# A Mixture-of-Experts Kernel: the First Pair of Expert Blocks Picked on TensorE Instead of Gathered from Memory

## The reference

```python
h = layer_norm(ALPHA * h + mixed, ln_g[i, 0], ln_b[i, 0])
ffn = hierarchical_moe(h, ...)              # 32 experts, top 2 of the chosen group of 8
h = layer_norm(ALPHA * h + ffn, ln_g[i, 1], ln_b[i, 1])
# inside hierarchical_moe, for the rows xb that chose expert e:
hb = silu(xb @ w_gate[e]) * (xb @ w_up[e])  # 1024 -> 512
y  = hb @ w_down[e]                         # 512 -> 1024
# y times its gate is added to the token's row
```

## Time and profile before

| what | value |
|---|---|
| median of 3 runs | 2321.19 us (2316.19 to 2324.91) |
| span of the profiled execution | 2316.0 us |
| mean granted TensorE clock | 0.955 of full speed |
| instructions | 28602 |
| TensorE matmul busy | 2117.5 us (91%) |
| DMA | 545.97 MB, mean 236 GB/s |
| expert blocks of layer 0 begin at | 1029.46 us of the span |
| expert blocks of layer 1 begin at | 1797.52 us of the span |

### The profile page before, as it was taken

How to read it: one execution, slowest core, us unless ns; L and a number is a source line. 1 busy time by engine, 2 the same in 40 slices (tenths; PEclk the granted TensorE clock), 3 DMA queues, 4 the chain that set the end, 5 groups by cost and what they waited for, 6 DMA issues and landing times. The chain is left out here.

```text
span 2316.0 us, 28602 instructions
## 1 busy us (share of the span) xinstructions
PE 2117.5 (91%) x11642; PEld 1217.9 (53%) x11642; DVE 693.5 (30%) x1536; ACT 539.4 (23%) x1241; POOL 253.4 (11%) x270
## 2 busy tenths in 40 slices
PE   7999999999999999969999899869996999989991
PEld 3446743434445687445555454457754555545550
DVE  1054325343555455542111010151125211101104
ACT  2123221033663145112221121130001212121111
POOL 0000000210101210101111111130000111111101
PEclk9999998999999999969999999979997999999996
DMA  9315242222011222169999999962034999999993
GB/s 348 125 59 186 85 181 94 78 105 73 1 56 58 91 77 76 35 241 406 423 424 423 423 423 417 389 244 98 30 125 177 373 422 425 423 423 423 423 407 141
DMA packets 100665, 545.97 MB, mean 236 GB/s; under 512 B 13377, under 2 KB 27498, under 8 KB 66587
## 3 DMA queue, kind: packets, MB, share of 16 engines
q1 hardware_dynamic: 80950, 504.17, 54.0%
q0 software_dynamic: 19232, 39.56, 4.8%
q10 hardware_dynamic: 340, 0.28, 0.0%
HBM read 538.86 MB, written 28.94 MB: 245 GB/s over the span
## 5 line engine op out<-in xcount | busy, mean ns | idle before, releaser
L759 PE MATMUL ps<-arena,ring 128*128 128x512 f32 (+8 forms) x1888 | 555.6, 456 | 11.1 <-DVE arena L2254 2.2
L759 PEld LDWEIGHTS ps<-arena,ring 128*128 128x128 f32 x1888 | 344.6, 193 | 212.8 <-issue 173.2
L1262 PE MATMUL ps<-ring,arena 128*64 128x256 f32 x3296 | 376.2, 384 | 5.0 <-ACT arena L1705 3.2
L1262 PEld LDWEIGHTS ps<-ring,arena 128*64 128x64 f32 x3296 | 234.4, 138 | 126.9 <-issue 4.9
L840 PE MATMUL ps<-ring,arena 128*128 128x512 f32 x528 | 233.1, 598 | 2.3 <-DVE arena L2082 1.2
L1275 PE MATMUL ps<-ring,arena 128*64 128x512 f32 x880 | 207.2, 615 | 24.2 <-DMA ring<-in_moe_w_down_dram 24.2
L2360 DVE SCALAR_TENSOR_TENSOR arena<-arena,ps 128x256 f32<-128x256 f32 x78 | 32.8, 421 | 565.3 <-ACT arena L1715 565.3
L1262 PE MATMUL ps<-arena 128*64 128x256 f32 x1696 | 192.6, 381 | 0.0
L2636 POOL DMA_INDIRECT assignment_rows<-arena x78 | 81.4, 1044 | 795.4 <-ACT arena L1721 752.3
L840 PEld LDWEIGHTS ps<-ring,arena 128*128 128x128 f32 x528 | 99.1, 191 | 123.7 <-issue 122.8
L1262 PEld LDWEIGHTS ps<-arena 128*64 128x64 f32 x1696 | 119.4, 137 | 60.5
(11 more groups left out here) (327 smaller groups left out, 1820.2 us busy)
## 6 DMA issues: line engine op xcount, KB each, us to landing
ring<-in_moe_w_down_dram SPq DMA_DIRECT2D x45, 2048.0 KB, 28.6
ring<-in_moe_w_up_dram SPq DMA_DIRECT2D x44, 2048.0 KB, 26.9
ring<-in_moe_w_gate_dram SPq DMA_DIRECT2D x43, 2048.0 KB, 24.7
arena<-in_moe_w_gate_dram SPq DMA_DIRECT2D x21, 2048.0 KB, 26.2
arena<-in_moe_w_up_dram SPq DMA_DIRECT2D x20, 2048.0 KB, 26.4
arena<-in_moe_w_down_dram SPq DMA_DIRECT2D x19, 2048.0 KB, 28.4
ring<-in_ada_w_dram SPq DMA_DIRECT2D x12, 2048.0 KB, 12.0
ring<-in_a_w_in_dram SPq DMA_DIRECT2D x12, 1536.0 KB, 14.8
```

What stands on the lines that cost most here:

```text
L759: ins = pe.matmul(dst, w, m, start=i == 0, stop=i == len(pairs) - 1)
L1262: ins = pe.matmul(ps[CAP * i:CAP * (i + 1), bank_, 256 * j:256 * (j + 1)], rows_t[:, k, :], w[:, k, 256 * i:256 * (i + 1)], start=k == 0, ...
```

## The change

The rows of the first pair are no longer gathered. For the two fixed experts the rank of a token within the expert is also its row in the block, so VectorE makes a one-hot matrix from the ranks, `chosen_rows` (per group of up to 128 tokens, 2 experts x 64 columns), with two instructions right behind the `ranks` job. TensorE multiplies the normed rows `X` (as the stationary operand, every eighth column) by it: eight chunks, each summed over the 5 (layer 0) or 4 (layer 1) groups of tokens. This picks and turns the rows in one product, into the first halves of banks 4 to 7. The first chunk stands ahead of the `order` product, the other seven behind it. All eight chunks are copied by ScalarE, which waits for them two by two.

The slot table's products move behind the gate product of block 0 and ahead of its up product, and write another bank. The gather of pair 0 and `turn_pair` 0 are gone; `turn_pair` 1 and its copy move from behind block 0 to behind block 1. Slab number 8 waits for the last chosen product instead of the gather.

```diff
-        block_hot = at(M0 + 1856, 10 * NBLK).rearrange("p (i b) -> p i b", b=NBLK)
+        chosen_rows = at(6144, 10 * CAP).rearrange("p (i j) -> p i j", j=CAP)
+        chosen_at = at(M0 + 352, 10).rearrange("p (t e) -> p t e", e=FIXED)
+        block_hot = at(M0 + 3072, 10 * NBLK).rearrange("p (i b) -> p i b", b=NBLK)
...
+        def chosen_pair(c):
+            return ps[:, 4 + c // 2, P * (c % 2):P * (c % 2 + 1)]
...
@@ SP, experts
-                        sp.wait_ge(xe_landed[NPR * l % 2], 16 * (NPR * l // 2 + 1))
+                        sp.wait_ge(xt_done, NPR * l + 1)
@@ TensorE, route
+                def chosen(c):
+                    for t in tiles:
+                        r = rows_of(t)
+                        ins = pe.matmul(chosen_pair(c), X[0:r, t, c:D:DC], chosen_rows[0:r, FIXED * t:FIXED * (t + 1), :],
+                                        start=t == 0, stop=t == tiles[-1])
+                    if c % 2:
+                        ins.then_inc(chunk_chosen if c < DC - 1 else xt_done, 1)
+                pe.wait_ge(chosen_ready, l + 1)
+                chosen(0)
                 pe.wait_ge(above_ready, l + 1)
                 b0, _ = begin(f"order{l}")
                 end(product(b0[:, 0:NE], [(ones_h[0:NE, :], above[0:NE, :])]))
-                b0, _ = begin(f"table{l}")
+                for c in range(1, DC):
+                    chosen(c)
+            def table(l):
+                _, b0 = begin(f"table{l}")
...
@@ TensorE, block_in
-                if n == 0:
-                    pe.wait_ge(xet_half, l + 1)
                 wide(expert_slab(tg, 0), 0, rows_t, 2 + B % 2).then_inc(gate_done, 1)
+                if n == 0:
+                    table(l)
                 landed(pe, tu)
@@ TensorE, experts
-                turn_pair(l, 0)
                 for n in range(NBS):
                     block_in(l, n)
-                    if n == 0:
+                    if n == 1:
                         turn_pair(l, 1)
@@ ScalarE, xet_copy
-                last = DC // 2 if j == 0 else DC
-                for c in range(last):
+                for c in range(DC):
+                    if j == 0:
+                        act.wait_ge(*((chunk_chosen, 3 * l + c // 2 + 1) if c < DC - 2 else (xt_done, J + 1)))
+                    src = turned_pair(n)[:, c, :] if j else chosen_pair(c)
@@ ScalarE, experts
-                    if B == NBS * l:
+                    if B == NBS * l + 1:
                         xet_copy(l, 1)
@@ VectorE, route, behind done(vec, "ranks")
+                vec.wait_ge(numbers_set, 9)
+                step(vec.scalar_tensor_tensor(chosen_at[:, 0:nt, :], ohb[:, 0:nt, 0:FIXED], -float(EMPTY), c[:, :, 0:FIXED], ALU.mult, ALU.add))
+                vec.scalar_tensor_tensor(chosen_rows[:, 0:FIXED * nt, :], spread(column_no[:, 0:CAP], 1, FIXED * nt), -float(EMPTY),
+                                         spread(chosen_at[:, 0:nt, :].rearrange("p t e -> p (t e)"), 2, CAP), ALU.add, ALU.is_equal)\
+                   .then_inc(chosen_ready, 1)
@@ VectorE, experts
-                vec.wait_ge(row_cols_in, 64)
-                first_rows(l)
@@ POOL, experts
                 pool.wait_ge(tok_ready, 4 * l + 2)
-                for j in range(2):
-                    gather(l, j)
+                gather(l, 1)
                 pool.wait_ge(tok_ready, 4 * l + 4)
                 gather(l, 2)
```

More of the change, by code:

```diff
@@ L489, in build @@
         xe_landed = [sem(f"xe_landed{i}") for i in range(2)]
-        xt_done, xet_copied, xet_half = sem("xt_done"), sem("xet_copied"), sem("xet_half")
+        xt_done, xet_copied = sem("xt_done"), sem("xet_copied")
+        chosen_ready, chunk_chosen = sem("chosen_ready"), sem("chunk_chosen")
         gu_ready, tanh_ready, hs_ready, tg_ready, hb_ready, y_ready, yo_ready = (
@@ L555, in pair_rows, with gathered @@
             return P if 2 * j + 1 < NBS else CAP
+        def gathered(J):
+            return J // 2 + 1 - (J // NPR + 1) * (J % 2 == 0)
+        def chosen_pair(c):
+            return ps[:, 4 + c // 2, P * (c % 2):P * (c % 2 + 1)]
         def turned_pair(n):
@@ L1240, in route @@
                 end(product(b0[:, 0:NE], [(ones_h[0:NE, :], above[0:NE, :])]))
-                b0, _ = begin(f"table{l}")
-                n = 2 * len(tiles)
+                for c in range(1, DC):
+                    chosen(c)
+            def table(l):
+                _, b0 = begin(f"table{l}")
+                n = 2 * (5 if l == 0 else 4)
                 pe.wait_ge(numbers_set, 9)
@@ L1281, in turn_pair @@
                 J = NPR * l + j
-                pe.wait_ge(xe_landed[J % 2], 16 * (J // 2 + 1))
+                pe.wait_ge(xe_landed[J % 2], 16 * gathered(J))
                 if J:
@@ L1699, in xet_copy @@
                 J, n = NPR * l + j, pair_rows(j)
-                act.wait_ge(xt_done, J + 1)
+                if j:
+                    act.wait_ge(xt_done, J + 1)
                 if J >= 2:
                     act.wait_ge(gu_ready, NBS * l + max(0, 2 * j - 2))
-                last = DC // 2 if j == 0 else DC
-                for c in range(last):
-                    ins = act.activation(xeT[J % 2][:, c, 0:n], turned_pair(n)[:, c, :], ACT.Identity, scale=row_cols[:, l, 0, c:c + 1],
+                for c in range(DC):
+                    if j == 0:
+                        act.wait_ge(*((chunk_chosen, 3 * l + c // 2 + 1) if c < DC - 2 else (xt_done, J + 1)))
+                    src = turned_pair(n)[:, c, :] if j else chosen_pair(c)
+                    ins = act.activation(xeT[J % 2][:, c, 0:n], src, ACT.Identity, scale=row_cols[:, l, 0, c:c + 1],
                                          bias=row_cols[:, l, 1, c:c + 1])
-                    if c < last - 1:
+                    if c < DC - 1:
                         mark(ins)
@@ L1723, in experts @@
             def experts(l):
+                act.wait_ge(row_cols_in, 64)
                 xet_copy(l, 0)
@@ L2338, in route @@
                 done(vec, name)
-                step(vec.tensor_copy(slot_tok, job_bank(name, NBLK)))
+                by_slot = ps[:, bank(name) + 1, 0:NBLK]
+                step(vec.tensor_copy(slot_tok, by_slot))
                 lo, hi = slice(0, CAP), slice(CAP, P)
@@ L2342, in route @@
                 vec.tensor_scalar(pair_tok[hi, 0:NBS // 2], slot_tok[hi, 1:NBS:2], 1, None, ALU.arith_shift_right).then_inc(tok_ready, 1)
-                free(vec.tensor_copy(emptied, job_bank(name, NBLK)), name)
+                free(vec.tensor_copy(emptied, by_slot), name)
                 taken(vec, name)
@@ L2406, in alpha @@
                 vec.scalar_tensor_tensor(x, lnp[0:r, 1, :], ALPHA, x, ALU.mult, ALU.add).then_inc(alpha_done, 1)
[L2408 to L2416, removed]
             def combine(l, t, between=None):
```

## The result

The changed kernel takes 2327.12 us in the median of 6 runs (2326.06 to 2331.6), the kernel before 2320.43 us (6 runs). The ratio is 1.0033, with a 95% interval of 1.002 to 1.0046: slower by 6.7 us by the medians, and by 7.7 us by the ratio, where 13 us faster was forecast. Half a per cent was what I called distinguishable, so it falls within "same", but the interval leaves no doubt of the sign. In the profiled execution the span grew from 2316.0 to 2325.7 us.

A forecast was written before the change was run, and what follows sets the result against it. Weight-slab traffic was taken to bound each mixture layer's second part, TensorE deciding when slab 14 goes out. Gains of 5.95 us (layer 0) and 7.0 (layer 1) sum to 13: median 2308.2 us, range 2301 to 2321.

The forecast's parts named there:

- What decides: Mixture layers: weight traffic binds their second part, so slab 14's issue decides; 5.95 us earlier in layer 0, 7.9 in layer 1.
- I take 0.245: Chosen products on TensorE: each two-record product costs 0.245 us at the full clock, despite the strided stationary operand.
- The sentence on the rule: Chosen products' loads: a 32-byte stride could make them dear, 0.65 us each, median 2332; deciding from 0.49; chance 0.12.
- I take 5.2 us: Routing on TensorE: the clock rises to full 5.2 us after the chosen products begin, 6.1 kept for the range.
- Rival 3: Both layers' routing: clock stays at 0.50 during the chosen products; median about 2323, no change; chance 0.08.
- VectorE's instructions: Start of routing, behind the ranks: the two added instructions take 0.2 and 0.85 us in layer 0.
- Slab 6: Layer 0's routing: this weight slab goes out 2.25 us later, at 1014.3 instead of 1012.08.
- The table: Slot table's products, now in TensorE's path after the gate product: 2.6 us in layer 0, 2.15 in layer 1.
- `turn_pair` 1: Transposes moved behind block 1, ahead of slab 14: they cost their full 0.98 us there, without a wait.
- The clock already high at the gate product: Block 0's first products in each layer: they run at full clock, saving 2.55 us.
- The gather of pair 1 in time: Mixture layer start: the gather has 10.9 us to land and takes 9 to 10, so costs nothing.
- The queue absorbs layer 0: Slab queue up to slab 14: layer 0's 0.6 us of excess disappears in 1.9 us of slack.

The follow-up runs named there:

- the first version: Changed kernel with chosen products reading neighbouring columns, matching weights and scales, and layer 0's last group over 128 rows; 2309.83 us, ratio 0.9956 to the kernel before.
- the version with both edits: Changed kernel reading neighbouring columns (weights not matched, wrong features) and 128 rows in layer 0's last group; one run 2314.23 us beside 2320.0.
- the version with filler: Mended kernel (neighbouring columns, 128 rows, all chunks behind the order product) plus constant products while TensorE waits; 2303.64 us, ratio 0.9944 to the kernel before.
- the last three versions: Changed kernel with neighbouring columns, matching weights and 128 rows; then also order product first; then also constant products during waits: 2309.83, 2309.7, 2303.64 us.

## Why the prediction was wrong

- **What decides (slab 14, the start of each mixture layer): right.** The two stretches account for 6.7 us of the loss of 6.7 to 7.7; with the faults mended they give 13.0 us, of which the first version keeps 10.6 in its trace and 10.2 by the ratio (8.8 by the medians).
- **The step that failed: "I take 0.245".** I took the price of a chosen product from contiguous two-record products and the harmlessness of the stride from transposes, one-record products. The chosen ones cost 0.48 at the full clock and 0.56 to 0.6 at the lower, where I had 0.46. Layer 1 shows the size: 53.31 against 47.59 us, 5.7 us for the stride. In layer 0, with the clock mended, it is 57.78 against 49.63, 8.2 us. The sentence on the rule had named this, and I weighed it at 0.12. Its price of 0.65 a product was too high, and its point of decision, 0.49, was where layer 1 came out: 15.98 us for 32 products. The price also rested on a wrong reading: the 326 ns of line 1249 came from the lower clock and not from a slow operand. Those loads, from layer 0 of the trace before, and the same ones in the trace after, where the table runs at the full clock:

```profile
L1249 PEld LDWEIGHTS ps<-arena x20: 283/333/333, 1015.2 to 1019.4; 128*128 128x128 f32 x16, 16*128 16x128 f32 x4
```

```profile
L1275 PEld LDWEIGHTS ps<-arena x20: 181/192/192, 1042.1 to 1044.4; 128*128 128x128 f32 x16, 16*128 16x128 f32 x4
```

- **The second failure: "I take 5.2 us" for the clock.** It held roughly in layer 1 (5.8 us) and not in layer 0, where the last group of 16 rows kept the clock at 0.50. Its cost is 63.72 - 57.78 = 5.9 us. Rival 3 had the effect in both layers and gave it no cause. With the slow loads alone the kernel would have stood at 1.0008.
- **The two together** turned 13 us of gain into a loss: 5.7 + 8.2 + 5.9 = 19.8 us lie between the version with both edits and the change. No rival held both, and the range did not reach it.
- **VectorE's instructions:** 0.17 and 0.82 us against 0.2 and 0.85. **Slab 6:** 2.76 us later against 2.25.
- **The table:** 2.85 and 2.28 us from start to start against 2.6 and 2.15. **`turn_pair` 1:** 1.09 us against 0.98, without a wait. **The clock already high at the gate product:** true in layer 1, false in layer 0 (5.54 us).
- **The gather of pair 1 in time:** right in the change, 0.6 us late in layer 1 once the path is as short as forecast.
- **The queue absorbs layer 0:** wrong in the first mended version, where it takes 1.3 us back; nothing clear of the scatter shows in layer 1, where I had subtracted 0.9.
- **The sum without the faults:** 5.81 + 7.31 against 5.95 + 7.9 forecast for slab 14. The sum is close in part because two errors cancel: the gate products come 7.5 and 9.1 us earlier instead of 7.0 and 8.5, and the way from there to slab 14 grows by 1.7 and 1.8 us instead of 1.05 and 0.6 (0.6 of it in layer 1 is the late gather).

## What to carry to other kernels

Price a product by a row of the same form: the same number of records, the same stride of the stationary operand. Transposes told nothing of two-record float32 products; where a row of the form is missing, that is the widest term, and the range must hold it. When products stand where the engine had been idle, ask in each stretch whether the clock will rise, and look for products of fewer rows among them: extending one over rows that multiply zeros cost nothing here and gave 5.9 us. When a stretch is shortened, see what was started in it: slab 6 behind the longer chain took 1.3 us of the gain back.

## What the runs showed of the hardware

- In the two-record float32 products a load of 128 x 128 takes about 335 ns at 32 bytes between elements and 329 at 16, against 198 at 8 and 192 for neighbouring elements, at the full clock, and the product follows the load (0.48 us against 0.24). At the lower clock all of them take 330 to 338 ns. The eight transposes with the same 32 bytes started 0.1225 us apart.
- A product over 16 or 64 rows among products over 128 rows brings a pause of 0.22 us on either side at the lower clock. In every layer 0 with such products in each chunk (the change, neighbouring columns, 64 rows, every second and every fourth column) the clock stayed at 0.50 for over 20 us of busy TensorE; in the seven with only 128-row chosen products there it rose 3.6 to 5.0 us after the first one. In layer 1, where all chosen products have 128 rows, it rose 4.0 to 6.4 us after the first in the versions without filler. These times scatter between traces of the same code: 4.0 to 5.8 us in the six whose layer 1 is that of the change.
- After it had risen, the clock fell again just behind a pause of 1.2 us before the order product in the version with filler, where TensorE had been busy for 0.89 of 2 us.
- The ranks of layer 0 stand between 1006.9 and 1015.0 us in the traces of this study, and what stands ahead of them is the same in all, but for the filler and, in the last three versions, the order in which the slabs of experts 0 and 1 are loaded. This is why the stretches are measured from there, and why single times were not used to rank the versions.
